# Reordering the attention turn of a hybrid layer: values three steps behind and next to the scores, three transpose banks, the k cache loaded tile by tile

## The reference, cut to what matters

```python
def sb_block(qb, qpos, k, v):
    # A[t,s] = sigmoid(z_ts) * prod_{s<j<t} (1 - sigmoid(z_tj)), s < t
    z = jnp.einsum('bhtd,bhsd->bhts', qb, k) * SB_SCALE
    mask = (kpos[None, :] < qpos[:, None])[None, None]
    log_keep = jnp.where(mask, jax.nn.log_sigmoid(-z), 0.0)
    after = lax.cumsum(log_keep, axis=3, reverse=True) - log_keep
    w = jnp.where(mask, jnp.exp(jax.nn.log_sigmoid(z) + after), 0.0)
    return jnp.einsum('bhts,bhsd->bhtd', w, v)
```

## Time and profile before

| what | us |
|---|---|
| median of 3 runs (lowest to highest) | 2797.46 (2793.91 to 2799.0) |
| the profiled execution, its own time | 2794.93 |
| its span in the trace | 2793.1 |
| PE busy in it | 2657.0 (95%) |
| DVE, ACT, POOL busy | 1516.6, 852.8, 364.8 |

### The profile page before, as it was taken

One profiled execution on the slowest core, in us unless ns is written; L12 is line 12 of the kernel. 1 busy time (PEld: TensorE's weight loads), 2 busy tenths in 40 slices (PEclk: granted clock), 3 DMA queues, 4 the chain that ended last, 5 costly groups with the idle time before them and its releaser, 6 DMA issues. The chain is left out here.

```text
span 2793.1 us, 48014 instructions
## 1 busy us (share of the span) xinstructions
PE 2657.0 (95%) x17088; PEld 2505.2 (90%) x17088; DVE 1516.6 (54%) x2581; ACT 852.8 (31%) x1566; POOL 364.8 (13%) x327
## 2 busy tenths in 40 slices
PE   6999999999996999999979999999999999999797
PEld 6888888888876998999979999999999999999697
DVE  4565655655572665666663443454444444454745
ACT  4443333433342343434342122211111111111533
POOL 0222322322240101111110002100000000000300
PEclk8999999999997999999989999999999999999799
DMA  5444444455532243335535433411111111111012
GB/s 138 91 90 82 98 91 97 84 81 92 88 78 47 33 75 55 73 52 78 56 137 196 161 116 122 139 43 41 45 38 45 38 45 38 45 44 38 29 38 93
DMA packets 331854, 214.31 MB, mean 77 GB/s; under 512 B 117828, under 2 KB 312216, under 8 KB 331672
## 3 DMA queue, kind: packets, MB, share of 16 engines
q1 hardware_dynamic: 331672, 211.98, 33.0%
HBM read 164.51 MB, written 47.41 MB: 76 GB/s over the span
## 5 line engine op out<-in xcount | busy, mean ns | idle before, releaser
L162 PE MATMUL bank<-operand_hi,w_hi 128*128 128x384 f32 x1584 | 533.4, 337 | 1.8 <-DVE w_lo L144 1.5
L162 PE MATMUL bank<-operand_hi,w_lo 128*128 128x384 f32 x1584 | 530.6, 335 | 0.0
L162 PE MATMUL bank<-operand_lo,w_hi 128*128 128x384 f32 x1584 | 530.5, 335 | 0.0
L137 ACT ACTIVATE w_hi<-w_raw 128x1024 fp32r<-128x1024 f32 x171 | 180.7, 1057 | 793.4 <-PE bank L162 489.8
L1051 POOL TENSOR_TENSOR wgt<-wgt,left 128x128 f32<-128x128 f32 (+2 forms) x224 | 227.2, 1025 | 596.8 <-DVE left L1006 366.5
L162 PEld LDWEIGHTS bank<-operand_hi,w_hi 128*128 128x128 f32 x1584 | 297.8, 188 | 2.6 <-issue 2.4
L144 DVE TENSOR_TENSOR w_lo<-w_raw,w_hi 128x1024 fp32r<-128x1024 f32 x171 | 211.7, 1238 | 160.8 <-ACT w_hi L137 159.7
L162 PEld LDWEIGHTS bank<-operand_lo,w_hi 128*128 128x128 f32 x1584 | 297.9, 188 | 0.3
L162 PEld LDWEIGHTS bank<-operand_hi,w_lo 128*128 128x128 f32 x1584 | 297.7, 188 | 0.0
L677 PE MATMUL acc<-operand_hi,w_hi 128*128 128x384 f32 x792 | 290.7, 367 | 5.5 <-PEq L212 5.5
L162 PE MATMUL sacc<-operand_hi,w_hi 128*128 128x384 f32 x768 | 268.3, 349 | 5.5 <-DVE w_lo L144 3.9
(11 more groups left out here) (319 smaller groups left out, 4467.9 us busy)
## 6 DMA issues: line engine op xcount, KB each, us to landing
w_raw<-in_w_in SPq DMA_DIRECT2D x65, 512.0 KB, 8.8
k_cache<-in_cache_k SPq DMA_DIRECT2D x256, 64.0 KB, 2.1
v_cache<-in_cache_v SPq DMA_DIRECT2D x64, 256.0 KB, 5.0
w_raw<-in_w_gate SPq DMA_DIRECT2D x22, 512.0 KB, 3.8
w_raw<-in_w_up SPq DMA_DIRECT2D x22, 512.0 KB, 3.9
w_raw<-in_w_down SPq DMA_DIRECT2D x22, 512.0 KB, 3.8
s_gate_a<-gate SPq DMA_DIRECT2D x24, 192.0 KB, 1.9
s_o<-o_t SPq DMA_DIRECT2D x8, 576.0 KB, 10.1
```

Of the source, the lines that this page charges most:

```text
L137: act.activation(S.w_hi[u0 % 2][:, :], S.raw[u0 % 2][:, :], ACT.Copy).then_inc(S.hi_done, 1)
L162: last = pe.matmul(acc[:, 0:RBN], w[:, k, :], a[:, k, rows], start=(n == 0), stop=(n == 3 * kts - 1 and more is None))
```

## The change

A turn has 17 steps in place of 16. On PE a step is now: the scores of unit s, right behind them the values of unit s - 3, the cache tile, the sample output, both slots of fill (with rows behind each), and last the transposes of unit s - 1. There are three `tp` banks, used in turn, and an event waits for the one three places earlier; in return the values have one bank. The order of `tp` events and DVE's order follow. The second sample unit moves ahead of block 7. The cache tiles are turned in steps 0 to 3 and 7 to 10; each buffer has a semaphore of its own and its next tile is loaded, by four DMAs, as soon as it is free. Work and data are otherwise the same.

```diff
@@ double_units
-        if t == 4:
-            out.append(("s", 0))
-    return out + [("s", 1)]
+        if t in (4, 6):
+            out.append(("s", (t - 4) // 2))
+    return out
@@
-STEPS = ND + 2
+LAG = 3
+STEPS = ND + LAG
-CACHE_AT = {1: 0, 2: 1, 3: 2, 4: 3, 8: 4, 9: 5, 10: 6, 11: 7}
-TURN_AT = {S_AT[0] + 3: 0, S_AT[1] + 2: 1}
+CACHE_AT = {0: 0, 1: 1, 2: 2, 3: 3, 7: 4, 8: 5, 9: 6, 10: 7}
+TURN_AT = {d + LAG + 1: j for j, d in enumerate(S_AT)}
-O_BANKS = [("p", t) for t in range(5)] + [("s", 0)] + [("p", t) for t in range(5, PT)] + [("s", 1)]
+O_BANKS = [("p", t) for t in range(5)] + [("s", 0), ("p", 5), ("p", 6), ("s", 1), ("p", 7)]
@@ tp_events: cache and o first, then the rows of both slots, then the two "w"
+    def bank_free(self, ev):
+        return self.tp(ev) - (3 if TP[self.last].index(ev) >= 2 else 2)
@@ stage_pairs
-        tp = [bank("tp0"), bank("tp1")]
-        ob = [bank("o0"), bank("o1")]
-        kc_in, vc_in, o_stored = sem("kc_in"), sem("vc_in"), sem("o_st")
+        tp = [bank("tp0"), bank("tp1"), bank("tp2")]
+        ob = bank("o")
+        kc_in, vc_in, o_stored = [sem(f"kc_in{n}") for n in range(4)], sem("vc_in"), sem("o_st")
@@ SP
-                        if s == 5:
-                            cache_k(t.i, 1, t.tp(("cache", 3)))
+                        if s in CACHE_AT:
+                            b = CACHE_AT[s]
+                            if b < 4 or not t.last:
+                                sp.wait_ge(S.tp_done, t.tp(("cache", b)))
+                                cache_k(t.i if b < 4 else t.i + 1, (b + 4) % 8)
-                        if s == 12 and not t.last:
-                            cache_k(t.i + 1, 0, t.tp(("cache", 7)))
                     sp.wait_ge(S.tp_drained, t.tp(("o", 1)))
+                    sp.wait_ge(S.o_read, HEAD + NO * (t.i + 1))
@@ PE
-                    pe.wait_ge(S.tp_drained, t.tp(ev) - 2)
-                    return tp[TP[t.last].index(ev) % 2]
+                    pe.wait_ge(S.tp_drained, t.bank_free(ev))
+                    return tp[TP[t.last].index(ev) % 3]
-                            pe.wait_ge(S.o_read, HEAD + NO * t.i + o_bank(d) - 1)
+                            pe.wait_ge(S.o_read, HEAD + NO * t.i + o_bank(d))
@@ PE, the step
                             scores(t, s)
-                        fill(t, 2 * s)
-                        rows_of(t, 2 * s)
-                        if 0 <= s - 2 < ND:
-                            values(t, s - 2)
-                        if 0 <= s - 1 < ND:
-                            transposes(t, s - 1)
-                        fill(t, 2 * s + 1)
-                        rows_of(t, 2 * s + 1)
+                        if 0 <= s - LAG < ND:
+                            values(t, s - LAG)
                         if s in CACHE_AT:
                             cache_t(t, CACHE_AT[s])
                         if s in TURN_AT:
                             turn_o(t, TURN_AT[s])
+                        fill(t, 2 * s)
+                        rows_of(t, 2 * s)
+                        fill(t, 2 * s + 1)
+                        rows_of(t, 2 * s + 1)
+                        if 0 <= s - 1 < ND:
+                            transposes(t, s - 1)
@@ DVE, the step
                             scan(t, 2 * s)
-                        for ev in ROWS_AT[t.last][2 * s]:
-                            drain(t, ev)
-                        if s < ND:
-                            scan(t, 2 * s + 1)
-                        if 0 <= s - 1 < ND:
-                            drain(t, ("w", 2 * s - 2))
-                            drain(t, ("w", 2 * s - 1))
-                        for ev in ROWS_AT[t.last][2 * s + 1]:
-                            drain(t, ev)
                         if s in CACHE_AT:
                             drain(t, ("cache", CACHE_AT[s]))
                         if s in TURN_AT:
                             drain(t, ("o", TURN_AT[s]))
+                        if s < ND:
+                            scan(t, 2 * s + 1)
+                        for ev in ROWS_AT[t.last][2 * s] + ROWS_AT[t.last][2 * s + 1]:
+                            drain(t, ev)
+                        if 0 <= s - 1 < ND:
+                            drain(t, ("w", 2 * s - 2))
+                            drain(t, ("w", 2 * s - 1))
```

More of the change, by code:

```diff
@@ L485, in tp_events @@
             ev.append(("o", TURN_AT[s]))
+        ev += ROWS_AT[last][2 * s]
+        ev += ROWS_AT[last][2 * s + 1]
+        if 0 <= s - 1 < ND:
+            ev += [("w", 2 * s - 2), ("w", 2 * s - 1)]
     return ev
@@ L512, in stage_pairs @@
     N = NH // 2
-    assert NTP % 2 == 0 and NO % 2 == 0 and NU % 4 == 0 and N % 2 == 0, (NTP, NO, NU)
+    assert NTP % 3 == 2 and NO % 2 == 0 and NU % 4 == 0 and N % 2 == 0, (NTP, NO, NU)
     with ExitStack() as ctx:
@@ L591, in _, with cache_k @@
                     sp.nop().then_inc(s, DMA_HEAD)
[L593 to L599, removed]
+                def cache_k(i, b):
+                    for s in range(4):
+                        src = A.cache_k[0, b, ds(2 * i, 2)].rearrange("h (s p) d -> s p h d", s=4)[s]
+                        sp.dma_start(kc[:, b % 4, s, :, :], src).then_inc(kc_in[b % 4], 16)
                 def cache_v(t, j):
@@ L638, in weight @@
                     S.W.load(sp, u0 + PRE_TILES + 4 + j, 4, t.i, src)
-                cache_k(0, 0, None)
+                for b in range(4):
+                    cache_k(0, b)
                 for j, (p, n) in enumerate(((1, 1), (0, 2), (1, 3))):
@@ L693, in turn_rows @@
                     src = stage[m % 2] if n is None else stage[STAGE_OF[m]]
-                    out = tp[(m if n is None else n) % 2]
+                    out = tp[m % 2 if n is None else n % 3]
                     for r in range(3):
@@ L700, in rows_of @@
                     for ev in ROWS_AT[t.last][slot]:
-                        turn_rows(ev, TP[t.last].index(ev), b_end(t.i, KV.index(ev)), t.tp(ev) - 2)
+                        turn_rows(ev, TP[t.last].index(ev), b_end(t.i, KV.index(ev)), t.bank_free(ev))
                 def open_tp(t, ev):
-                    pe.wait_ge(S.tp_drained, t.tp(ev) - 2)
-                    return tp[TP[t.last].index(ev) % 2]
+                    pe.wait_ge(S.tp_drained, t.bank_free(ev))
+                    return tp[TP[t.last].index(ev) % 3]
                 def cache_t(t, b):
-                    pe.wait_ge(kc_in, 512 * t.i + 256 * (b // 4 + 1))
+                    pe.wait_ge(kc_in[b % 4], 128 * t.i + 64 * (b // 4 + 1))
                     out = open_tp(t, ("cache", b))
@@ L761, in values @@
                     pe.wait_ge(S.tp_drained, t.tp(("w", u + 1)))
-                    o = ob[o_bank(d) % 2]
+                    o = ob
                     w0, w1 = w_t[u % 4], w_t[u % 4 + 1]
@@ L912, in read_o @@
                     kind, r = DU[d][:2]
-                    src = ob[o_bank(d) % 2]
+                    src = ob
                     if kind == "p":
@@ L929, in _ @@
                             sigmoids(t, 2 * s + 1)
-                        if 0 <= s - 2 < ND and (DU[s - 2][0] == "s" or DU[s - 2][5]):
-                            read_o(t, s - 2)
+                        if 0 <= s - LAG < ND and (DU[s - LAG][0] == "s" or DU[s - LAG][5]):
+                            read_o(t, s - LAG)
                         for m in BLOCKS_AT[t.last][s]:
@@ L964, in drain @@
                 def drain(t, ev):
-                    src = tp[TP[t.last].index(ev) % 2]
+                    src = tp[TP[t.last].index(ev) % 3]
                     kind, x = ev
```

7 lines of the change are left out of this document (2 added, 5 removed).

## The result

The changed kernel takes 2757.21 us in the median of four runs (2755.53 to 2764.65), the kernel before 2795.68 (2793.36 to 2799.0). The ratio is 0.9869, its 95% interval 0.9851 to 0.9886. The profiled execution took 2755.53 us, 39.4 less than the one of before.

What follows compares the result with a forecast made beforehand. PE, busy for 95% of the span, was taken as the bound. Terms of 7.0 + 3.4 + 12.0 + 5.0 = 27.4 us, against the median of 2797.46, gave 2770 us, range 2763 to 2783.

Steps and rivals of the forecast that it cites:

- The pauses at the loop: PE's two pauses at a turn's start, where the hardware loop goes round: 5.4 us, expected to stay, no gain.
- Part 1: Three `tp` banks: PE's waits before transposes go, 7.0 us in the first seven turns, 3.4 us in the last.
- Part 2: PE's order: fewer fill starts and passages between full-array and half-array matmuls, 1.5 us a turn, 12.0 us for eight.
- Rival 1: Joining fills on PE saves nothing, only passages between matmul kinds count: 4.3 us from the order, 2778 us; chance 0.16.
- Part 3: Values three steps behind: ACT's late `read_o`, PE's wait for it and the half clock behind go, 5.0 us.
- Part 4: K cache loaded by tiles: counted at nothing; without the cover of steps, one load in PE's way costs 2.1 us.
- Part 5: One bank for values: ACT reads the last values before PE needs the bank again, so it costs nothing.
- rival 2: PE waits for weights drained by DVE instead of banks, so the banks' 10.4 us stay: 2780 us; chance 0.11.
- rival 3: The single value bank binds because ACT reads late, 80 places; at 0.5 us each 2810 us; chance 0.06.

Runs made afterwards that it cites:

- banks: Kernel before with three `tp` banks and one bank for values, all else as before; 2776.23 us, ratio 0.994.
- late_wait: late_values plus a PE wait, behind the turn's last slot of fill, for ACT's read of the last values; 2764.78 us, ratio 0.9897.
- late_values: Changed kernel with the turn's last values between the two slots of fill, not ahead of them; 2762.43 us, ratio 0.9884.
- values_apart: Changed kernel with a slot of fill between scores and values; 2771.42 us, ratio 0.9923.
- sample_first: Kernel before with the second sample unit ahead of block 7 and its cache tiles a step earlier; 2809.26 us, ratio 1.0055.
- turn_last: Changed kernel with the second sample unit's output turned as the last thing of a turn; 2761.64 us, ratio 0.9881.
- two_banks: Changed kernel with two `tp` and two value banks as before; 2787.65 us, ratio 0.9974.
- lots: Changed kernel with the k cache loaded in lots of four tiles, in steps 5 and 12, PE waiting for whole lots; 2850.49 us, ratio 1.0205.
- after_again: Changed kernel measured once more, nothing altered; 2758.61 us, ratio 0.9874.
- lag2: Changed kernel with values two steps behind the scores instead of three, 16 steps a turn; 2792.63 us, ratio 0.9996.

## Why the prediction was wrong

**The pauses at the loop: the step that failed.** The prediction said that they "lie where the hardware loop goes round, name no engine that was really late, and stay". The first half is right, the "stay" is not, and the price of nothing is the term that failed. They went from 3.08 and 2.87 us to 1.38 and 1.26, and with them went 10.2 us of half clock, 8.4 us in all. With that term the forecast would have been 2761.6 and the range, moved as a whole, 2754.6 to 2774.6, with the measured 2757.2 in it. The branch has a row of its own in the sequencer's records (minimum, median, maximum in ns of three passages), shown for PE's queue and ACT's in the kernel before, and for PE's in the changed one:

```profile
L572 PEldq COMPARE_BRANCH  x3: 83/3497/3763, 270.7 to 664.9; - x3
...
L572 ACTq COMPARE_BRANCH  x3: 40/45/45, 272.2 to 666.4; - x3
```

```profile
L577 PEldq COMPARE_BRANCH  x3: 83/3430/3547, 262.3 to 636.0; - x3
```

PE's branch takes 3.8 and 3.5 us where the loop goes round and 0.08 us at its end; ACT's takes 0.04. In all twelve traces with the loop it took 3.3 to 3.8. The sequencer issues ahead of the matmuls, so part of the branch is hidden, and the pause is what is left. The table has the time by which the branch begins before the modelled end of the last matmul (the lead), how long the branch takes, and the distance between matmuls, for the first and the second passage:

| run | lead, us | branch, us | distance, us | half clock behind, us |
|---|---|---|---|---|
| before | 1.23 | 3.76, 3.50 | 3.08, 2.87 | 6.8, 3.4 |
| 1, banks | 1.34 | 3.65, 3.42 | 2.86, 2.62 | 3.4, none |
| 9, late_wait | 0.77 | 3.43, 3.59 | 3.27, 3.42 | 3.4, 6.8 |
| 8, late_values | 2.21 | 3.81, 3.80 | 2.22, 2.19 | none |
| 4, values_apart | 2.21 | 3.36, 3.29 | 1.76, 1.69 | none |
| 6, sample_first | 2.47 | 3.81, 3.80 | 1.95, 1.93 | none |
| 7, turn_last | 2.76 | 3.57, 3.59 | 1.35, 1.37 | none |
| 2, two_banks | 2.77 | 3.35, 3.39 | 1.19, 1.22 | none |
| 5, lots | 2.78 | 3.67, 3.30 | 1.58, 1.13 | none |
| changed kernel | 2.78 | 3.55, 3.43 | 1.38, 1.26 | none |
| 12, after_again | 2.78 | 3.49, 3.75 | 1.32, 1.58 | none |
| 3, lag2 | 3.30 | 3.33, 3.29 | 0.64, 0.60 | none |

In all 24 passages the distance is the branch's length less the lead, plus 0.54 to 0.69 us, of which 0.27 to 0.34 is the last matmul's own length. So the two numbers of the branch account for the pause, and DVE's `q_lo`, to which the wait view of the earlier trace rows puts it down, is not needed.

In the kernel before, the last thing in a turn, the transpose of the sample output, waited for ACT to read values computed nine matmuls earlier:

```profile
270.17 0.28 ACT L919 ACTIVATE o_sample<-o 128x128 f32<-128x128 f32 x1 [3.07 <-PE o L781]
```

ACT was in time for the matmuls, so no wait of PE showed, but the sequencer could not run ahead: it came to its branch at 270.69 us, right behind this read, when the last matmul ended at 271.92. The change moved the second sample unit ahead, so this wait is long met when the sequencer gets there. sample_first shows that in the kernel before, and late_wait against late_values turns the lead on and off by one wait. The Trainium skill, Runtime: NRT & Kernel Launch, Instruction fetch mechanics, says that a taken branch whose target lies outside the fetched window has to fetch it first. That agrees with 3.5 us for PE when the branch is taken and 0.08 us when it falls through; the fetch itself was not tested apart from the branch.

**Part 1, three banks:** right in kind, too small. 14 us (banks) against 10.4. I summed the idle time that the waits view names, not the delay of the next start: in the earlier trace rows two groups of two transposes start 1.45 us apart, where two transposes take 0.2.

**Part 2, fewer groups:** right. The order adds 2.7 - 1.3 = 1.4 us to the banks' gain in a turn, against 1.5; in the last turn 1.3. The whole gives 11 us against 12. Rival 1, only passages count, has fallen: it has 4.3 us for the order, against 11 here, and 4 to 5 for values_apart, against 14. The start of a fill is a price of its own.

**Part 3, the read of o:** half right. ACT's long wait for the `o_t` store shrank to 3.3 us at most, with no wait of PE behind it. But the seventh turn, which took 5.3 us more than its neighbours, still takes 4.0 more (96.9 instead of 92.9), since DVE now stands there for another store. The row of DVE (its idle time before, and the releaser):

```profile
691.20 0.56 DVE L962 COPY v_rows<-tp 128x384 f32<-128x384 f32 x1 [4.14 <-DMA out_new_v_prompt<-kv_out]
```

PE's 2.3 us before the cache tile and 3.4 us at half clock follow. The 5.0 us turned into some 3, of which this turn gave 1.3 and the sixth 1.6. The sixth lost them behind a wait of the same kind, in which ACT stood 4.7 us for the store, at 585 us; that is the part of the term that held. The cause of the seventh turn's disturbance was not tested and stays open. It is not there in the two kernels without a loop, nor in two_banks and values_apart.

**Part 4 and Part 5:** right at nothing. No run shows PE waiting for a k cache tile with loads by tile, and for the value bank with a lag of three one does, late_wait, once for 0.2 us. The price in case the cover is gone was far off: I gave 2.1 us for one load, and it is 9 us and more in each of seven turns (lots), since the loads don't come alone but behind other stores.

**The other rivals.** The wait did not move to DVE's weights at lag three (rival 2); at lag two it does, and takes the gain. The single value bank never bound in the changed kernel (rival 3).

So the sum, term by term, with the forecast's in brackets: banks 14.0 (10.4), order 11.0 (12.0), disturbances about 3 (5.0), loop 8.4 (0), together 36.4 against 27.4, for 36.5 in the stretch. The first three come to 28.0 against 27.4; that they agree so well is luck, since a term that was too small offsets two that were too large. The lower end of the range was no bound of the terms either: Part 2 at its 14 us gives 2768, and 2763 counts Part 3's 5 us a second time.

## What to carry to other kernels

Where a hardware loop closes on the busiest engine, look at what its sequencer waits for last, not only at what the engine waits for: a wait that never delays a matmul can still keep the branch from being hidden. Price a wait by the delay of the next instruction's start. When work is moved earlier, look at each queue that feeds it, because a load in a batch behind unrelated stores is as late as the last of them.

## What was not expected of the hardware

PE's taken branch took 3.3 to 3.8 us in 24 passages, those of the other engines 0.04 to 0.06. Behind distances of 2.86 us and more at the loop (five passages) the clock was granted at half for 3.4 or 6.8 us; behind the other 19, of 2.62 us and less, it was not. The length alone does not decide it: in the seventh turn the clock was at half for 3.4 us behind a distance of 2.54 us in the changed kernel and of 2.31 in turn_last, and not behind 2.35 us in late_values. The first matmul of a fill group is followed 0.08 to 0.11 us later than the pitch of 0.174 us, behind transposes, masks, scores and values alike. Writing the loop out also made the SSD stage 6 to 9 us faster, which stays unexplained.
